# A hybrid diffusion step on one core: weight slots planned anew, 15 of them, and the load order from a time model

## The reference

```python
for i in range(DEPTH):
    kind = i % 3                       # 0 windowed attention, 1 with normalised q/k, 2 latent attention
    sh1, sc1, g1, sh2, sc2, g2 = adaln(c, w_mod[i], b_mod[i])   # silu(c) @ w_mod: 1024 x 6144, 24 MB a layer
    h = rmsnorm(x, norm_mix[i]) * (1 + sc1) + sh1
    x = x + g1 * mixer(h)                                  # wqkv 6 MB and wo 4 MB, or the latent set
    h = rmsnorm(x, norm_ffn[i]) * (1 + sc2) + sh2
    x = x + g2 * moe(h)                                    # 16 x (w_gate, w_up, w_down), 1 MB each: 48 MB a layer
```

## Time and profile before

| | us |
|---|---|
| median of 3 runs | 1651.51 |
| the profiled execution | 1663.96 |
| its span | 1662.2 |
| TensorE busy / VectorE / ScalarE / GpSimd | 1446.6 / 545.1 / 372.3 / 196.9 |
| granted TensorE clock, mean | 0.951 |
| DMA | 428.68 MB, 258 GB/s over the span |

### The profile page before, as it was taken

The page is one execution under the profiler, slowest core; times in us unless marked ns, Lnnn a source line. Parts: engine busy times, 40 slices in busy tenths (PEclk is TensorE's granted clock), DMA queues, the critical chain, the costliest instruction groups (busy, mean ns, idle before and its releaser), DMA issues.

```text
span 1662.2 us, 26392 instructions
## 1 busy us (share of the span) xinstructions
PE 1446.6 (87%) x10704; PEld 857.0 (52%) x10704; DVE 545.1 (33%) x1329; ACT 372.3 (22%) x985; POOL 196.9 (12%) x286
## 2 busy tenths in 40 slices
PE   3989997998897998898989999979889899969982
PEld 1866674332676686332464456743327566843321
DVE  0126523211526625111522343332115257242114
ACT  1105421111212612111120342301102036121110
POOL 0100021101113022000110000210011000220011
PEclk9989998999999999999989999999989999979996
DMA  9996235999869126999958224379996940539992
GB/s 339 349 318 230 88 116 211 408 420 415 282 231 324 23 105 230 373 420 422 345 183 263 36 77 177 102 293 416 421 411 201 310 159 2 203 121 406 421 379 87
DMA packets 125027, 428.68 MB, mean 258 GB/s; under 512 B 13099, under 2 KB 55038, under 8 KB 100326
## 3 DMA queue, kind: packets, MB, share of 16 engines
q1 hardware_dynamic: 96854, 350.32, 54.9%
q0 software_dynamic: 21104, 72.71, 12.7%
q10 hardware_dynamic: 6944, 3.91, 0.8%
HBM read 389.20 MB, written 40.26 MB: 258 GB/s over the span
## 4 chain that ended last, share of the span: by engine, by line
PE 67%; DMA 12%; DVE 8%; issue 5%; ACT 3%; POOL 2%; another core or an unknown queue 2%; SPq 1%; DVEq 0%; ACTq 0%; POOLq 0%
PE bank L1681 59%; DMA work<-in_moe_w_gate 5%; DMA ring<-in_w_mod 4%; PE bank L1851 3%; DMA h_slots<-xn,row_of 2%; PE bank L2015 2%; ACT pp L1022 2%; PE bank L1738 1%; POOL small L698 1%; POOL h_slots L801 1%; DVE xn L1169 1%; DMA hT<-h_slots 1%; PE bank L1898 1%; SPq L606 1%
## 5 line engine op out<-in xcount | busy, mean ns | idle before, releaser
L1681 PE MATMUL bank<-ring,pp 128*32 128x512 f32 x2312 | 317.4, 597 | 14.0 <-issue 11.9
L1681 PE MATMUL bank<-ring,hT 128*128 128x256 f32 (+3 forms) x1142 | 272.2, 398 | 5.9 <-issue 3.3
L1681 PEld LDWEIGHTS bank<-ring,hT 128*128 128x128 f32 x1142 | 213.6, 196 | 62.7 <-issue 32.1
L1681 PE MATMUL bank<-work,pp 128*32 128x512 f32 x888 | 241.9, 628 | 3.0 <-DVE pp L1555 2.3
L1681 PE MATMUL bank<-ring,xn 128*128 128x256 f32 x768 | 168.2, 380 | 0.0
L1681 PEld LDWEIGHTS bank<-ring,pp 128*32 128x32 f32 x2312 | 87.4, 110 | 135.5 <-issue 134.5
L1681 PEld LDWEIGHTS bank<-ring,xn 128*128 128x128 f32 x768 | 145.0, 190 | 19.4
L1681 PE MATMUL bank<-V,pp 128*32 128x512 f32 x640 | 124.3, 634 | 30.5 <-issue 21.3
L1571 DVE TENSOR_TENSOR pp<-bank,pp 128x256 f32<-128x256 f32 x40 | 17.0, 425 | 340.1 <-ACT pp L1099 340.1
L1681 PE MATMUL bank<-ring,condT 128*32 128x256 f32 x1536 | 99.0, 404 | 17.0 <-DMA ring<-in_w_mod 17.0
L1022 ACT ACTIVATE pp<-bank,neg_max 128x384 f32<-128x384 f32 x192 | 96.7, 524 | 13.2 <-DVE neg_max L1462 10.1
(11 more groups left out here) (254 smaller groups left out, 1561.2 us busy)
## 6 DMA issues: line engine op xcount, KB each, us to landing
ring<-in_w_mod SPq DMA_DIRECT2D x96, 1024.0 KB, 8.2
ring<-in_moe_w_down SPq DMA_DIRECT2D x52, 1024.0 KB, 19.0
ring<-in_moe_w_gate SPq DMA_DIRECT2D x32, 1024.0 KB, 15.1
ring<-in_moe_w_up SPq DMA_DIRECT2D x32, 1024.0 KB, 17.5
hT<-h_slots POOLq DMA_DIRECT2D x36, 512.0 KB, 11.4
V<-in_moe_w_gate SPq DMA_DIRECT2D x16, 1024.0 KB, 13.9
V<-in_moe_w_up SPq DMA_DIRECT2D x16, 1024.0 KB, 16.3
work<-in_moe_w_gate SPq DMA_DIRECT2D x16, 1024.0 KB, 10.0
```

The costliest lines, as they stand in the source:

```text
L1681: return pe.matmul(out, lhsT, rhs, start=start, stop=stop)
```

## The change

It replaces the planner and the order of SP's fills and gives the plan two more slots, 13 and 14: the two halves of `gbc`. `V` is packed for kinds 0 and 1 (`Vg`, four blocks of 256 in its first quarter), so slot 9 can hold mixer weights there. The experts' down matrices lose slots 4 and 5 and get slot 13, for places that end before block 7; gate/up pairs of places 4 and up get (4, 5) as a fifth pair. `wo` and the route units may use slots 4 to 7 only. SP's single order comes out of the plan: fill by fill the unit that can start earliest by the model's clock, among the next 16 in the order of use. GpSimd waits for the last mixer unit of slot 13 or 14 before it loads a gate there, and for the last expert unit of slot 13 before the gathers of L840. The zero rows are written ahead of the first expert fill of layer 0, from `V`; the waits for them in attention go. The two early vectors of the next layer are summed in banks 4 and 5, and the wait for their copies moves from ahead of `gather_rows` to the first down product.

```diff
+LOAD_SPAN, LOAD_SPAN_MOE, AHEAD = 2.45, 2.8, 16
...
+        mark["held", L], mark["rows", L] = now + 70.0, now + 82.0
+        now += 76.0
         for e in range(E):
-            ends["moe_g", L, e] = ends["moe_u", L, e] = now + 12.0 * last_block(e) + 7.0
-            ends["moe_d", L, e] = now + 12.0 * last_block(e) + 23.0
...
+            for part in ("moe_g", "moe_u"):
+                begin[part, L, e], end[part, L, e] = now + 11.8 * first_block(e), now + 11.8 * last_block(e) + 7.5
+            begin["moe_d", L, e] = now + 11.8 * first_block(e) + 11.0
+            end["moe_d", L, e] = now + 11.8 * last_block(e) + 18.5
...
+def homes(key):
+
+    name, (L, phase) = key[0], phase_of(key)
+    if name in ("moe_g", "moe_u"):
+        pairs = ((0, 1), (2, 3), (8, 9), (10, 11)) + (((4, 5),) if key[2] >= FIXED else ())
+        return [pair if name == "moe_g" else pair[1:] for pair in pairs]
+    if name == "moe_d":
+        return [(slot,) for slot in (6, 7, 12) + ((13,) if last_block(key[2]) < 7 else ())]
+    if name == "wo" or phase == "route":
+        return [(slot,) for slot in (4, 5, 6, 7)]
+    if name == "ukv":
+        return [(2,), (3,)]
+    if name == "mod" and key[2] < 2:
+        return [(slot,) for slot in range(R)]
+    return [(slot,) for slot in tuple(range(R)) + ((9, 13, 14) if KINDS[L] < 2 else (13, 14))]
...
+    def opens(key):
+        name, phase = key[0], phase_of(key)
+        if name[:3] == "moe" and key[2] >= FIXED:
+            return mark["rows", phase[0]]
+        return 0.0
+
+    def choice(key):
+        if key[0] == "moe_u":
+            return None
+        phase = phase_of(key)
+        free = {home: max(max(free_at[s], home_opens(s, phase, mark)) for s in home) for home in homes(key)}
+        best = min(free, key=free.get)
+        at = max(free[best], opens(key))
+        safe = [k for k in waiting if k != key and not (key[0] == "moe_g" and k == ("moe_u",) + key[1:])]
+        return (at, best) if not safe or at <= min(begin[k] for k in safe) else None
...
+    while waiting:
+        found = []
+        for n, key in enumerate(waiting[:AHEAD]):
+            c = choice(key)
+            if c:
+                found.append((max(c[0], now), n, key, c[1]))
+        at, _, key, home = min(found)
+        span = LOAD_SPAN_MOE if key[0][:3] == "moe" and key[2] >= FIXED else LOAD_SPAN
+        now = at + span * len(home)
+        take(key, home[0])
+        if key[0] == "moe_g":
+            take(("moe_u",) + key[1:], home[1])
...
+            def home_free(slot, L, part):
+
+                if part == "main" and L > 0:
+                    if slot == 9:
+                        sp.wait_ge(mixed, L)
+                    elif slot == 13:
+                        sp.wait_ge(comb_used, 3 * L - 1)
+                    elif slot == 14:
+                        sp.wait_ge(x_moe_v, 3 * L)
+                elif part == "moe":
+                    if slot == 13:
+                        sp.wait_ge(wo_mul, 12 * (L + 1))
+                    elif slot in (10, 11) and KINDS[L] < 2:
+                        wait_evacuated(sp, *[("qT", L, p) for p in range(8)], *[("kT", L, g) for g in range(G)])
+                        sp.wait_ge(states, 32 * (L + 1))
+                    elif slot >= R:
+                        sp.wait_ge(o_ready, 8 * (L + 1))
+                        sp.wait_ge(states, 32 * (L + 1))
...
+                if (L, FIXED) not in held_at and e >= FIXED:
+                    sp.wait_ge(held_ready, L + 1)
+                    sp.wait_ge(g_in[1], 16 * (BLOCKS // 2 * L + 1))
...
+                pool.wait_ge(slot_used[13], released(13, *phases_to(L, "main")))
                 load_gate(L, 0)
                 load_columns(L, 1)
+                pool.wait_ge(slot_used[14], released(14, *phases_to(L, "main")))
                 load_gate(L, 1)
...
-                out = bank[6 + at % 2]
+                out = mod_bank(v)
...
-                pe.wait_ge(mod_copied, min(6 * L + 8, 24))
...
+                    if blk == 0:
+                        pe.wait_ge(mod_copied, min(6 * L + 8, 24))
```

More of the change, by code:

```diff
@@ L156, in ends_in @@
     return [i for i in range(E) if last_block(i) == blk]
-def moe_units(L):
-    units = []
-    for i in range(E):
-        units += [(4 * first_block(i), ("moe_g", L, i)), (4 * first_block(i), ("moe_u", L, i)),
-                  (4 * first_block(i) + 5, ("moe_d", L, i))]
-    units = [key for _, key in sorted(units, key=lambda u: u[0])]
-    return units[:4] + mod_units(L)["route"][4:] + units[4:]
-def unit_ends():
-    ends, now = {}, 0.0
-    def pass_mods(units, now):
+PROJ_LANES = {"dq": (3.5, 1.8), "dkv": (3.5, 0.7)}
@@ L174, in pass_mods, with unit_times, run, run_mods @@
+ATT_SPAN = (56.0, 45.0, 101.0, 56.0)
+LOAD_SPAN, LOAD_SPAN_MOE, AHEAD = 2.45, 2.8, 16
+def unit_times():
+    begin, end, mark = {}, {}, {}
+    def run(key, now, span):
+        begin[key], end[key] = now, now + span
+        return now + span
+    def run_mods(units, now):
         for key in units:
-            now += 1.0
-            ends[key] = now
-        return now
-    now = pass_mods([("mod", 0, v, q) for v in range(2) for q in range(4)], now)
+            now = run(key, now, 0.95)
+        return now
+    run_mods([("mod", 0, v, q) for v in range(2) for q in range(4)], 25.0)
+    now = 38.0
@@ new lines, in unit_times, with phase_of @@
+        now += 11.8 * BLOCKS + 20.0
+        mark["summed", L] = now
+    return begin, end, mark
+def phase_of(key):
+    name, L = key[0], key[1]
+    if name[:3] == "moe":
+        return L, "moe"
+    return (L - 1, "route") if name == "mod" and key[2] < 2 and L > 0 else (L, "main")
+def homes(key):
[12 more added lines that the diff above has]
+    return [(slot,) for slot in tuple(range(R)) + ((9, 13, 14) if KINDS[L] < 2 else (13, 14))]
@@ new lines, in home_opens @@
+def home_opens(slot, phase, mark):
+    L, part = phase
+    if part == "moe":
+        late = {13: "mixed_in", 8: "heads", 9: "heads", 12: "heads"}
+        if slot in (10, 11):
+            return mark["turned" if KINDS[L] < 2 else "heads", L]
+        return mark[late[slot], L] if slot in late else 0.0
+    return mark["summed", L - 1] if part == "main" and slot in (9, 13, 14) and L > 0 else 0.0
+def plan_ring():
+    begin, end, mark = unit_times()
+    waiting = sorted(begin, key=lambda key: (begin[key], end[key]))
+    place, order, fills, free_at, now = {}, [], [0] * SLOT_COUNT, [0.0] * SLOT_COUNT, 0.0
+    def opens(key):
[12 more added lines that the diff above has]
+        return (at, best) if not safe or at <= min(begin[k] for k in safe) else None
@@ L468, in unit, with released, phases_to, mod_bank @@
             return slots(ring_place[key][0], 1)[:, 0, :]
+        def released(slot, *phases):
+            return 1 + sum(1 for key, (home, _) in ring_place.items() if home == slot and phase_of(key) in phases)
+        def phases_to(L, part):
+            parts = ("main", "route", "moe")
+            return [(l, q) for l in range(L + 1) for q in parts if l < L or parts.index(q) <= parts.index(part)]
         def mod_at(L, v):
             return 6 * L + v
+        def mod_bank(v):
+            return bank[4 + v if v < 2 else 6 + v % 2]
         def mods_done(units):
@@ L614, in fill_mod @@
                 fill(key, src.rearrange("(k p) n -> p k n", p=P), 2 * D, 2)
-            for slot in range(13):
+            for slot in range(SLOT_COUNT):
                 sp.sem_inc(slot_used[slot], 1)
```

208 lines of the change are left out of this document (101 added, 107 removed).

## The result

The changed kernel is slower. In the runs that follow the change it took 1669.95 us (median of four, 1669.52 to 1671.86), the kernel before beside it 1653.72: a ratio of 1.0099, interval 1.0070 to 1.0129. In a later job on another chip it was 1668.58 against 1656.90, 1.0058 (1.0039 to 1.0076). I had forecast 1625.

The account below looks back on a forecast made before the run. TensorE, 87% busy, was taken to lose time to weights arriving in bursts, with slots, not bytes, stopping the prefetch. Mixers -23.8, routing -3, experts 0 gave -27, from 1651.5 to 1625 us; 8-in-10 range 1600 to 1649.

Parts of the forecast that it names:

- Mixers: Waits for modulation units in the mixers of layers 0, 1 and 3 all go: -23.8 us, bounds 0 to 26.
- mixer waits elsewhere: Sign of a wrong forecast: TensorE waits at other mixer places because SP stands at a slot that opens late.
- Routing: Attention's end to block 1: early experts loaded sooner, route units limited to slots 4 to 7; -3 us, bounds -12 to +8.
- Expert stages: Expert blocks: blocks 8 and 9 start earlier, given back at the end; 0 per layer, bounds -10 to +8.
- the two standstills at T+11.8 and T+23.8: SP waits for down slots of places 4 and 5, until T+11.7 and T+23.7; T is block 1's gate/up start.
- the new wait at block 9's down product: The last down unit must take a slot of block 8, so TensorE stands 4.1 us.
- T+126.5 and T+129: Two estimates of when TensorE goes on after the expert stage, counted from block 1's gate/up start; before, T+127.9.
- the 4 us for SP's two standstills: Allowance in the count for block 8's start: T-3+28*3.18+4 = T+90, 2.7 earlier than before.
- A: Rival, expert stages: bytes alone count, each stage wins about 8 us; 1591, or 1608 for half; chance 0.20.
- B: Rival, mixers: VectorE's head work swallows the gain in layers 1 and 3, route units cost more; 1648, chance 0.12.
- C: Rival, expert stages: SP's single order makes DMA stand at down slots, 35 us in all; 1660, chance 0.11.
- D: Rival, whole plan: it does what the kernel before did, new slots idle; 1651, chance 0.05.

Follow-up runs that it names:

- e_ukv: Changed kernel with layer 2's fourth group of modulation units kept out of slots 2 and 3: 1656.48 us, 0.9974 of the kernel before.
- e_route: Changed kernel with the modulation units behind the routing allowed in slots 0 to 7, not only 4 to 7: 1668.64 us, 1.0071 of the kernel before.
- e_down: Changed kernel with down units of places 12 to 15 also allowed in slots 4 and 5: 1641.27 us, 0.9904 of the kernel before.
- e_best: Changed kernel with the planner's down-unit clock set to the trace and down units of places 12 to 15 allowed in slots 0 to 7 and 12: 1630.88 us, 0.9801.
- e_clock: Changed kernel with only the planner's clock for down units set to the trace (20.0 and 23.6 us, 12.0 a block): 1681.26 us, 1.0130 of the kernel before.

## Why the prediction was wrong, point by point

**Mixers, -23.8: half right.** Layers 0, 1 and 3 gave 10.0, 4.5 and 10.5 us in the first pair of profiles, where the steps said 9.6, 4.8 and 9.4. With eight slots the old waits are back, so the cause is among those given. In layer 1 and for the first wait of layer 3 it is the slots. In layer 0 the zero rows were no cause; slots and the later gate rows go together there, and in layer 3's later waits, and were not tried singly. What failed is layer 2, which had no term: the prediction read that its mixer had no such wait before ("none in layer 2") and asked no further. I had looked at which waits go, not at what the new plan puts behind what: a `ukv` unit may only lie in slots 2 and 3, and one of them was taken by a modulation unit that is read immediately before it. That is +12.9 us, shown by SP's rows and by e_ukv. It could have been found blind, by writing out the plan of layer 2 as I did for the experts of layer 0. The list of what would show the forecast wrong had "mixer waits elsewhere" only under SP standing at a slot that opens late; this is such a wait, at a slot that is used late.

**Routing, -3: wrong by 6.** It came to +3.5 over both pairs: -3.6 in layer 0, +3.8 and +3.6 in layers 1 and 2 in the first. The sum counted TensorE's wait for the route units, and these cost nothing: freed of them, TensorE stands for the rows (e_route). The stretch ends with the scatter and its read-back, and these are slower where something is loaded beside them: landing took 11.6, 12.3 and 11.9 us behind the last issue in layers 0 to 2, where the route units and two down units are under way, and 3.96 in layer 3, where they are not; before it was 13.7, 9.3, 10.3 and 4.1. The prediction allowed a microsecond for "the down units 2 and 3 beside the scatter"; the landing alone came 3.0 us later in layer 1 and 1.7 in layer 2 than before. The Trainium skill, DMA: Bandwidth & Descriptors (Issuing engines are not separate DMA queues), says that transfers of all issuing engines run interleaved on the same 16 DMA engines; these rows agree with that, and I had used it for bytes in the expert blocks instead of here. Which of the six loads delay the scatter by how much was not settled: holding the two down units back shortened the landing to 5.67 us and delayed the read-back instead.

**Expert stages, 0: wrong by 16.** The order, the two standstills at T+11.8 and T+23.8 and the new wait at block 9's down product came as written, the last at 4.76 us for a forecast 4.1. What failed is the value between the two ends, T+126.5 and T+129 against T+127.9 before: it rested on blocks 8 and 9 being earlier by enough to pay for the new wait. In layer 0 it was T+129.5 (408.90), the late end: block 8 came at T+93.6 and not at T+90 (T+92.7 before), block 9 at T+107.8 and not at T+104 (T+108.8 before). So of the 3.5 to 4.5 us that block 9 was to be early, 1.0 came. A mis-sized term is the 4 us for SP's two standstills: from T-2.5 to T+93.3 the DMA engines moved 37.07 MB at 387 GB/s, before, from T-3 to T+92.5, 39.44 MB at 413, and 26 GB/s less over 96 us is, by estimate, 6 us of loading. That places 2 of the 3.6 us by which block 8 missed its forecast; the rest is not placed. In the other layers the wait was larger still, 5.98, 4.82 and 7.88. Given a slot, the stages fall by 20 us (e_down), of which 16 were the loss.

**The rivals.** A (bytes alone) is false in a way worth keeping: starting the queue earlier, up to dropping its wait for rows altogether, took 6 us at most from the stages and nothing that could be measured from the time. B is false, no head work of VectorE took the mixers' gain. C forecast 1660 by standstills at down slots between T+36 and T+72; DMA was full there (421 GB/s at T+36 to T+48), the loss came at the two ends of the stage. Its time was nearest, its mechanism was not the one, though e_best shows that its cause, the planner's clock for down units, was worth some 10 us of the stages once the last unit had its slot (561.2 to 552.0; e_best also lets these units lie in slots 0 to 3). D is false.

**What stays open.** Why the trace of before is long in both its profiles, so that the traces show 5 us of difference and the medians 12 to 16. How layer 0's 10 us in the mixer divide between the slots and the later gate rows. And why the wait before block 8 is 5.2 to 5.5 us in nearly every layer of the kernels with the old order, with four pairs or five; the count of units above gives 2 us of it.

## What to carry to other kernels

When a planner replaces a hand-made order, write out its result for every layer and look at two things before any sum: what each unit with few possible places lies behind, and where the last unit of the stage lies; two late slots there, one in layer 2's mixer (13 us) and one at the end of each expert stage (16), cost as much as the new slots brought in the other three mixers. A planner's clock and its pools have to be mended together: the right clock alone made these stages 11 us longer, with the slots they are the shortest. And a wait that stands next to another transfer's landing has no price until the trace shows which of the two ends last.

## What the runs showed of the hardware that I had not expected

A load of 1 MB has no fixed price on SP. A 1 MB unit of expert weights mostly took 0.34 to 0.38 us, but the last down unit of e_clock took 4.44 (its rows above). Loads of `wqkv`, also 1 MB but cut as 256 columns out of a wide matrix, took 2.14 us for two in the same rows, and in the changed kernel 22.54 us for six:

```profile
399.60 22.54 SPq L673 DMA_DIRECT2D ring<-in_qkn_wqkv  x6
```

The last three of these six end at 416.4, 419.2 and 422.1, each within 0.2 us of the landing of a unit asked for before (416.39, 419.31, 422.26). That fits an SP that stands until the queue has room again; whether the cut of the load counts too was not tried. A small load behind such units is then late by their landings, as the last down unit of e_clock was.
